# Projection stage: transposed normalised rows from a channel-major copy of the input and a spread row of norms

## The reference

```python
def rmsnorm(x, w):
    xf = x.astype(F32)
    y = xf * lax.rsqrt(jnp.mean(xf * xf, axis=-1, keepdims=True) + RMS_EPS)
    return (y * w.astype(F32)).astype(x.dtype)

def split_proj(h, w_in, lb):
    z = h @ w_in
    qa, ka, va, qr, fr, ir, gr = jnp.split(z, SPLITS, axis=-1)
    ...

h = rmsnorm(yp, norm1_w[l])
qa, ka, va, qr, kr, logf, ir, gr = split_proj(h, w_in[l], lb)
```

## Time and profile before

| | |
|---|---|
| median of 3 runs | 3004.83 us (3002.6 to 3006.21) |
| the profiled execution, its own time | 3005.86 us |
| its span, first to last instruction | 3004.1 us |
| PE busy over the span | 2707.0 us (90%) |
| DVE busy | 1564.4 us (52%) |
| ACT busy | 972.5 us (32%) |
| POOL busy | 564.7 us (19%) |
| granted TensorE clock, mean | 0.958 |

### The profile page before, as it was taken

How to read it: one execution, slowest core, us unless ns; L and a number is a source line. 1 busy time by engine, 2 the same in 40 slices (tenths; PEclk the granted TensorE clock), 3 DMA queues, 4 the chain that set the end, 5 groups by cost and what they waited for, 6 DMA issues and landing times. The chain is left out here.

```text
span 3004.1 us, 39548 instructions
## 1 busy us (share of the span) xinstructions
PE 2707.0 (90%) x12065; PEld 1646.2 (55%) x12066; DVE 1564.4 (52%) x2999; ACT 972.5 (32%) x2178; POOL 564.7 (19%) x827
## 2 busy tenths in 40 slices
PE   8999999999999957889977999589999999999960
PEld 6677777777777644555564555334444444444420
DVE  2556556555656567888843555433333343333327
ACT  2333333333333325777734656100000000000008
POOL 2111111111111111222210111222222222222210
PEclk9999999999999968999988999799999999999985
DMA  6000010001000070000042222198777679696848
GB/s 239 32 32 25 24 38 35 24 24 38 31 28 25 21 236 15 12 8 8 8 142 85 91 84 84 50 382 309 270 277 277 213 247 320 224 318 232 282 170 301
DMA packets 204144, 395.19 MB, mean 132 GB/s; under 512 B 26643, under 2 KB 66835, under 8 KB 201889
## 3 DMA queue, kind: packets, MB, share of 16 engines
q1 hardware_dynamic: 152800, 333.75, 31.0%
q0 software_dynamic: 16704, 48.61, 4.5%
q10 hardware_dynamic: 34560, 11.84, 1.7%
HBM read 311.25 MB, written 71.08 MB: 127 GB/s over the span
## 5 line engine op out<-in xcount | busy, mean ns | idle before, releaser
L659 PE MATMUL z_psum<-w_in_sb,hT 128*128 128x512 f32 x1088 | 480.5, 593 | 0.0
L653 PE MATMUL z_psum<-hT,w_in_sb 128*128 128x128 f32 x3264 | 374.1, 276 | 0.8 <-ACT hT L329 0.8
L653 PEld LDWEIGHTS z_psum<-hT,w_in_sb 128*128 128x128 f32 x3264 | 369.9, 193 | 1.7 <-ACT hT L329 1.2
L1904 PE MATMUL gate_psum<-w_gate_sb,block_rows_T 128*128 x720 | 318.8, 596 | 19.7 <-DVE block_rows_T L1843 16.0
L1919 PE MATMUL down_psum<-w_down_sb,hidden_T 128*128 x720 | 319.1, 597 | 14.5 <-DVE hidden_T L1859 14.5
L659 PEld LDWEIGHTS z_psum<-w_in_sb,hT 128*128 128x128 f32 x1088 | 200.8, 191 | 220.7 <-issue 220.7
L1908 PE MATMUL up_psum<-w_up_sb,block_rows_T 128*128 x720 | 316.4, 593 | 0.0
L1817 ACT COPY block_out<-down_psum 128x512 f32<-128x512 f32 x45 | 26.3, 585 | 815.4 <-issue 804.8
L1614 PE MATMUL y_psum<-w_out_sb,mix_T 128*128 128x512 f32 x544 | 243.4, 601 | 0.9 <-DVE mix_T L1467 0.9
L1904 PEld LDWEIGHTS gate_psum<-w_gate_sb,block_rows_T 128*128 128x128 f32 x720 | 137.7, 192 | 193.3 <-issue 193.2
L1919 PEld LDWEIGHTS down_psum<-w_down_sb,hidden_T 128*128 128x128 f32 x720 | 137.2, 191 | 190.1 <-issue 190.1
(11 more groups left out here) (309 smaller groups left out, 3487.5 us busy)
## 6 DMA issues: line engine op xcount, KB each, us to landing
w_gate_sb<-in_w_e_gate SPq DMA_DIRECT2D x32, 2048.0 KB, 11.3
w_up_sb<-in_w_e_up SPq DMA_DIRECT2D x32, 2048.0 KB, 10.7
w_down_sb<-in_w_e_down SPq DMA_DIRECT2D x32, 2048.0 KB, 12.7
expert_rows<-scratch_moe SPq DMA_DIRECT2D x17, 1024.0 KB, 8.6
w_in_sb<-in_w_in SPq DMA_DIRECT2D x7, 2048.0 KB, 18.7
hidden_by_lane<-hidden ACTq DMA_DIRECT2D x720, 16.0 KB
scratch_z<-z_ring SPq DMA_DIRECT2D x34, 256.0 KB, 2.1
scratch_h<-h SPq DMA_DIRECT2D x17, 512.0 KB, 2.6
```

Source lines behind the costliest of these rows:

```text
L653: mm = pe.matmul(out[:, hd * P:(hd + 1) * P], w[:, c, col:col + P], hT[:, u, c, :], start=(c == 0), stop=(c == DC - 1))
L659: mm = pe.matmul(out[:, :], hT[:, u, c, :], w[:, c, g * HW:(g + 1) * HW], start=(c == 0), stop=(c == DC - 1))
L1904: mm = pe.matmul(gps[:, :], xT[:, u, c, :], part(wg, slot, c), start=(c == 0), stop=(c == DC - 1))
```

## The change

The host lays out x a second time, channel-major (`in_x_T`: for each tile 128 channels of a chunk on the partitions, chunks and rows along the free axis), and SP loads that tile too. The transposed normalised rows are then computed directly: ScalarE writes the 128 norms onto the diagonal of a 128x128 matrix (`rdiag`), TensorE multiplies a matrix of ones by it, so that every partition holds the row of norms (`spread_rstd`, one product in the place of the eight transposes), and VectorE makes `hT` by eight products, one for each chunk: transposed x times a column of `norm1_w` times the row of norms in PSUM (`make_hT`). They stand where VectorE's copy of half of `hT` stood. The product `make_h`, the eight transposes and both copies go. `norm1_w` is loaded as columns instead of a broadcast row.

```diff
-        n1 = sb("norm1_row", [P, D])
+        n1 = sb("norm1_cols", [P, DC])
...
-        h = sb("h_tile", [P, D])
+        xT = sb("x_tile_T", [P, DC, P])
+        ones = sb("ones_p1", [P, P])
+        rdiag = sb("rstd_diagonal", [P, P])
...
-        hps = ps("hT_psum", [P, 2, HW])
+        rps = ps("rstd_row_psum", [P, HW])
...
             def load_x(t):
 
-                wait(sp, h_ok, t)
+                wait(sp, rstd_ok, t)
                 sp.dma_start(x[:, :], xs if is_last(t) else row(xp, t)).then_inc(x_in, 16)
+                wait(sp, hT_ok, t)
+                sp.dma_start(xT[:, :, :].rearrange("p c t -> p (c t)"), row(dr["x_T"], t)).then_inc(xT_in, 16)
...
             def stats(t):
 
                 act.wait_ge(x_in, 16 * t + 16)
-                wait(act, h_ok, t)
+                wait(act, rd_ok, t)
...
-            def hT_copy(t, u):
-                act.wait_ge(hT_ps, t + 1)
-                nc.scalar.copy(hT[:, u, 0:4, :].rearrange("p c t -> p (c t)"), hps[:, 0, :]).then_inc(hT_act, 1)
+                act.wait_ge(rstd_ok, t + 1)
+                wait(act, rr_ps, t)
+                nc.scalar.activation(rdiag[:, :], ident[:, :], ACT.Copy, scale=st[:, 2:3]).then_inc(rd_ok, 1)
...
                 evac(t, u, FR)
-                if not is_last(t):
-                    hT_copy(t + 1, 1 - u)
...
-            def make_h(t):
-                dve.wait_ge(rstd_ok, t + 1)
-                wait(dve, hT_ps, t)
-                stt(out=h[:, :], in0=x[:, :], scalar=st[:, 2:3], in1=n1[:, :], op0=ALU.mult, op1=ALU.mult).then_inc(h_ok, 1)
-
-            def hT_copy(t, u):
-                dve.wait_ge(hT_ps, t + 1)
-                nc.vector.tensor_copy(hT[:, u, 4:8, :].rearrange("p c t -> p (c t)"), hps[:, 1, :]).then_inc(hT_dve, 1)
+            def make_hT(t, u):
+                dve.wait_ge(rr_ps, t + 1)
+                dve.wait_ge(xT_in, 16 * t + 16)
+                wait(dve, z_ps, 8 * t - 8)
+                for c in range(DC):
+                    ins = stt(out=hT[:, u, c, :], in0=xT[:, c, :], scalar=n1[:, c:c + 1], in1=rps[:, 0:P], op0=ALU.mult, op1=ALU.mult)
+                ins.then_inc(hT_ok, 1)
...
                 evac(t, u, KA)
-                if not is_last(t):
-                    make_h(t + 1)
...
                 forget(t, u)
                 if not is_last(t):
-                    hT_copy(t + 1, 1 - u)
+                    make_hT(t + 1, 1 - u)
...
-            def turn(t):
-                pe.wait_ge(h_ok, t + 1)
-                wait(pe, hT_act, t)
-                wait(pe, hT_dve, t)
-                for c in range(DC):
-                    mm = pe.transpose(hps[:, c // 4, (c % 4) * P:(c % 4 + 1) * P], h[:, c * P:(c + 1) * P], ident[:, :])
-                mm.then_inc(hT_ps, 1)
+            def spread_rstd(t):
+                pe.wait_ge(rd_ok, t + 1)
+                wait(pe, hT_ok, t)
+                pe.matmul(rps[:, 0:P], ones[:, :], rdiag[:, :], start=True, stop=True).then_inc(rr_ps, 1)
...
                     if j == KT and not is_last(t):
-                        turn(t + 1)
+                        spread_rstd(t + 1)
```

More of the change, by code:

```diff
@@ L167, in project @@
         act_step, dve_step, pool_step = sem("p1_act_step"), sem("p1_dve_step"), sem("p1_pool_step")
-        rstd_ok, h_ok, hT_ps = sem("rstd_ready"), sem("h_ready"), sem("hT_transposed")
-        hT_act, hT_dve = sem("hT_half0_ready"), sem("hT_half1_ready")
+        rstd_ok, rd_ok, rr_ps, hT_ok = sem("rstd_ready"), sem("rstd_diagonal_ready"), sem("rstd_row_in_psum"), sem("hT_ready")
+        xT_in, ones_ok = sem("x_T_loaded"), sem("ones_p1_ready")
         z_ps, z_act, z_dve = sem("z_in_psum"), sem("z_even_copied"), sem("z_odd_copied")
@@ L200, in load_x @@
             def load_x(t):
-                wait(sp, h_ok, t)
+                wait(sp, rstd_ok, t)
                 sp.dma_start(x[:, :], xs if is_last(t) else row(xp, t)).then_inc(x_in, 16)
+                wait(sp, hT_ok, t)
+                sp.dma_start(xT[:, :, :].rearrange("p c t -> p (c t)"), row(dr["x_T"], t)).then_inc(xT_in, 16)
             load_x(0)
-            sp.dma_start(n1[:, :], dr["norm1_w"].to_broadcast([P, D])).then_inc(n1_in, 16)
+            with nc.allow_non_contiguous_dma(reason="1024 floats, once"):
+                sp.dma_start(n1[:, :], dr["norm1_w"].rearrange("l (c p) -> p (l c)", p=P)).then_inc(n1_in, 16)
             sp.dma_start(gnrow[:, :], dr["gnorm_w"].to_broadcast([P, P])).then_inc(row_in, 16)
@@ L413, in _ @@
             stats(0)
-            hT_copy(0, 0)
             act.wait_ge(lb_e, 1)
@@ L572, in tile @@
                     state(g, v)
+            nc.vector.memset(ones[:, :], 1.0).then_inc(ones_ok, 1)
             dve.wait_ge(n1_in, 16)
-            make_h(0)
-            hT_copy(0, 0)
+            make_hT(0, 0)
             dve.wait_ge(row_in, 48)
@@ L707, in tile @@
             def tile(t, u, rec=True):
-                pe.wait_ge(hT_act, t + 1)
-                pe.wait_ge(hT_dve, t + 1)
+                pe.wait_ge(hT_ok, t + 1)
                 g, v = t - 1, 1 - u
@@ L727, in _ @@
             pe.wait_ge(consts["sem"], consts["n"])
-            turn(0)
+            pe.wait_ge(ones_ok, 1)
+            spread_rstd(0)
             tile(0, 0, False)
@@ L2076 @@
         dr[name] = nc.dram_tensor(f"in_{name}", a.shape, _mybir.dt.from_np(a.dtype), kind="ExternalInput").ap()
+    x_T = _np.concatenate([arrays["in_x_prompt"].reshape(SEQ, D), arrays["in_x_sample"].reshape(P, D)])
+    arrays["in_x_T"] = _np.ascontiguousarray(x_T.reshape(TILES, P, DC, P).transpose(0, 3, 2, 1).reshape(TILES, P, D))
+    dr["x_T"] = nc.dram_tensor("in_x_T", (TILES, P, D), F32, kind="ExternalInput").ap()
     for name, shape in _OUTS:
```

## The result

The changed kernel took 3020.06 us (median of 4 runs, 3017.56 to 3024.14), the kernel before 3003.72 us in the same series: a ratio of 1.0052, 95% interval 1.0037 to 1.0067. It is slower by 16.3 us; 3023 us was forecast, with a range of 3010 to 3034. The profiled execution was the shortest of the four, 3017.56 us.

A forecast was written before the change was run, and what follows sets the result against it. TensorE, busy 970.59 of 976.20 us, bounds the projection, waiting only for VectorE's level operands. Terms +19.5 - 0.5 - 1.0 = +18.0 us on 3005.86 give 3023.9; the median stands 1.03 lower: 3023 us, range 3010 to 3034.

The forecast's parts named there:

- The eight transposes that the change removes stand in a gap.: TensorE between levels 2 and 3: removal saves nothing in 15 tiles, the wait grows from 0.29 to about 0.93 us.
- +19.5 us for the products: VectorE after the forget gate: eight products replace a 0.60 us copy, delaying level 5; 1.30 us a tile, tiles 1 to 15.
- the list of waits: TensorE's waits for level operands: about 30, some 0.9 us ahead of level 3 and 1.2 us ahead of level 5.
- -0.5 us in tile 0: Tile 0, which has no level: TensorE's next group can start about 0.5 us before 39.82, after ScalarE's copy of VA.
- -1.0 us at the start: Launch, before the first group at 16.20: the new chain lets it start at 15.2; gain between 0 and 1.6 us.
- The edits at nothing: ScalarE's scaled copy in the statistics and SP's added 512 KB load a tile: no cost while their cover lasts.
- The sum: Whole program: +19.5 - 0.5 - 1.0 = +18.0 us on the profiled execution's 3005.86 us.
- One sign of being wrong: Outside the projection: the prediction called itself wrong if the time changed there; no size given.
- The saving was not kept: Rival, TensorE ahead of level 3: saving kept and products hidden behind the forget gate, 11.1 us less, 2994 us; chance 0.05.
- the products were not hidden: Rival, VectorE ahead of level 5: saving lost, products hidden by the slack, -1.5 us, 3003 us; chance 0.08.
- They did overlap: Rival, VectorE's eight products: they do not overlap at all, +27.6 us, 3032 us; chance 0.08.
- The granted clock did not fall at the two waits: Rival, TensorE after the two waits a tile: they cost it its pace, 43 us more, 3066 us; chance 0.02.

The follow-up runs named there:

- the run that only fills the gap: Kernel before, with its transposes and copies, and level 3 issued inside the FR group, against the kernel before: 2993.80 us, ratio 0.9964 (0.9952 to 0.9976).
- the changed kernel's second trace: The changed kernel run once more, unaltered, in one series with its version with eight idle transposes put back: 3019.46 us, ratio 1.0048 to the kernel before.
- the last kernel with idle transposes: Changed kernel with products ahead of the forget gate and level 3 inside the FR group, plus eight idle transposes in each tile's KT: 2999.24 us, ratio 0.9977.
- the one to keep: Changed kernel with products moved ahead of the forget gate and level 3 issued inside the FR group: 2977.67 us (0.9913), repeated at 2978.53 us (0.9912).

## Why the prediction was right, point by point

- **"The eight transposes that the change removes stand in a gap."** Shown from both sides: 2.64 us from level 2 to level 3 without them, 2.65 with eight put back, and 0.87 us a tile (0.65 less the new product) as soon as level 3 no longer stands behind them.
- **+19.5 us for the products.** The step was 0.259 us (0.2625 assumed from rows 6). Level 5 starts 8.32 us after the QR group does (538.14 to 546.46) instead of 7.15: 1.17 us later, where the sum had 1.20, and the group behind it comes 0.10 us later still, as assumed. A tile grew by 1.26 us, from 61.03 (495.11 to 556.14 in the trace before) to 62.29, where 1.30 was forecast; from the level 0 in tile 1 to the one in tile 16 it is 934.5 instead of 915.5 us, 19.0 us in 15 tiles. Moving the products took back 19.1 us. Only the list of waits differs from what was expected, 1.01 instead of 1.2 us ahead of level 5; the last section says why.
- **-0.5 us in tile 0, -1.0 us at the start.** The first was right, the second too large. In the trace before, group KA starts at 24.77; the run that only fills the gap has the same start as the kernel before, and the changed kernel's second trace the same start as its first. Group KA of the first of the three, then QA and KA of the two others:

```profile
24.77 13.90 PE L659 MATMUL z_psum<-w_in_sb,hT 128*128 128x512 f32 x32
...
15.34 9.82 PE L655 MATMUL z_psum<-hT,w_in_sb 128*128 128x128 f32 x64 [0.83 <-ACT hT L329]
24.99 13.90 PE L661 MATMUL z_psum<-w_in_sb,hT 128*128 128x512 f32 x32
...
15.09 9.20 PE L648 MATMUL z_psum<-hT,w_in_sb 128*128 128x128 f32 x64 [2.32 <-DVE hT L441]
24.13 13.90 PE L654 MATMUL z_psum<-w_in_sb,hT 128*128 128x512 f32 x32
```

  The timeline of the changed kernel's start in its first trace, to be read beside that and rows 9 and 10, from the scaled copy to QA, KA and FR of tile 0:

```profile
11.25 0.40 ACT L333 ACTIVATE rstd_diagonal<-ident,rms_stats 128x128 f32<-128x128 f32 x1
11.80 0.77 PE L629 MATMUL rstd_row_psum<-rstd_diagonal,ones_p 128*128 128x128 f32 x2 [11.80 <-ACT rstd_diagonal L333]
12.67 2.15 DVE L441 SCALAR_TENSOR_TENSOR hT<-x_tile_T,norm_cols,rstd_row_psum 128x128 f32<-128x128 f32 x8 [10.48 <-PE rstd_row_psum L629]
14.88 9.76 PE L648 MATMUL z_psum<-hT,w_in_sb 128*128 128x128 f32 x64 [2.32 <-DVE hT L441]
...
24.48 13.90 PE L654 MATMUL z_psum<-w_in_sb,hT 128*128 128x512 f32 x32
...
39.07 3.17 PE L648 MATMUL z_psum<-hT,w_in_sb 128*128 128x128 f32 x26
```

  From KA to FR it takes 14.59 us instead of 15.05: 0.46 us less in tile 0. QA starts 1.3 us earlier, at 14.88 instead of 16.20, but KA only 0.3 us: QA took 9.60 us where it had taken 8.57. What was gained in time was lost in pace. Other traces say how little of that is firm: KA starts at 24.08 to 25.35 us in the eight traces with the change's start and no idle work ahead, and at 24.77 and 24.99 in the two with the old start, so a gain at the start can't be told from none.
- **The edits at nothing.** The scaled copy took 0.40 us, and after the start, where the sum had it, nobody waited for it. SP issues the later weights from 16.94 us on instead of 14.07: the load of the second tile's x, begun at 11.24 instead of 13.31, is listed with 5.06 us instead of 0.72, and the new load follows it at 16.35. The prediction had set that load against x alone, not against the weights behind it; no group waited for its weights.
- **The sum.** Up to the level 0 in tile 1 the changed kernel gains 0.65 us (74.34 against 74.99), and in the 15 tiles it loses 19.0: that is the 18.4 us by which the stage's end moved, where 18.0 was forecast. The nearness has some luck in it, for 0.5 us too much in the tiles and 0.85 us too much gain ahead of them partly cancel. One sign of being wrong that the prediction names did appear: the profiled executions differ by 6.7 us outside the projection. It is within the range of the twelve traces there, 1951.7 to 1960.6 us from the last level 0 to the end; two traces of one kernel differ in it by 4.7 us; that the change has no part in it is argued from this spread, not shown. The same holds for the median, which moved by 16.3.
- **The rivals.** The saving was not kept, and the products were not hidden. They did overlap: eight whole durations of 342 ns would be 2.74 us, 2.07 were measured. The Trainium skill ("VectorE: DVE Perf Modes", section "The DRAIN you can't avoid") gives waiting for an empty pipe as the general rule, which is all that the prediction took from it, and adds in the same place that a next operation that is not held starts earlier. The trace agrees with the addition: the products start 0.259 us apart and last 0.34. The granted clock did not fall at the two waits, and the FR group behind the wait of 0.93 us takes 7.15 us up to the next level as before (529.66 to 536.81; 521.42 to 528.57).

## What to carry to other kernels

Work taken from the busiest engine saves time only if that engine is not about to wait: look up what releases it next, and whether that chain starts before or after the work that goes. Work moved to another engine costs where it stands in that engine's order, so compare the slack of the next thing waited for with what is added, and look in the same order for an idle stretch that could take it. Here the same instructions gave +16 us in one place, 0 in another, and, once the gap was closed too, -0.9%, of which closing the gap alone gives 0.4%.

## What the runs showed that I had not expected

- A wait costs TensorE more than the idle time that the profile lists. Listed waits of 0.29, 0.92 and 1.01 us shortened or lengthened a tile by 0.55, 1.19 and 1.26 us: 0.25 to 0.27 us more each time. The rows show both parts. A level is listed with 1.05 us though the next group starts 0.89 us after it, so some 0.16 us of the tail in front of a wait count as busy; and behind a wait the level takes 1.16 us, 0.10 more. The loads of weights in the trace before show the second: level 2's first weights are loaded at 517.35, 0.43 us ahead of its first product, level 3's, behind the wait, at 520.43 together with it.
- An earlier start bought next to nothing, because TensorE's first group ran slowly: its 64 instructions took 9.04 to 10.07 us in the eight traces with two instructions ahead of them, 8.57 and 9.65 us in the two with eight transposes, and 7.25 us in both traces behind 64 idle instructions and two real ones. So enough work ahead removes the slowness; that eight transposes help more than two products is not shown. The granted clock is given as 1.00 (2.4 GHz) in all these stretches, so that column does not show it, though the eight transposes of rows 10 start 0.21 us apart and those of rows 9 0.11.
- Runs of one kernel can differ by some 10 us: 2998.51 to 3010.92 us for the kernel before in one series, 2990.45 to 3004.37 for the last kernel with idle transposes. Others hardly differ: 3017.66 to 3020.52 for the changed kernel, 2977.95 to 2980.16 for the one to keep. Where a trace of a long run was kept, the difference lies outside the projection. What decides it is open.
